# Stick-breaking attention, last head pair: the six copies of the output's inputs go two by two over three tiles instead of three by three over two, and the output units' pieces run a tile later

## The reference, cut to what matters

```python
y_pool = pool_mixer(u, w_pool[i], pool_scale[i])          # 512 channels, done before the attention
o_sb = stick_breaking_attention(q, k, v)                  # 8 heads of 64
y_sb = rms_norm_2(o_sb, ones).reshape(b, s, SB_WIDTH) * g_sb[i]
mix = jnp.concatenate([y_pool, y_sb], axis=-1) @ w_out[i]
h = h + rms_norm_2(mix, g_mix_post[i])
```

## Time and profile before

| | us |
|---|---|
| median of 3 runs | 2429.26 (2428.68 to 2429.6) |
| profiled execution, time | 2429.0 |
| profiled execution, span of the core | 2427.2 |
| PE busy in the span | 2298.8 (95%) |
| DVE, POOL, ACT busy | 1605.5, 1170.5, 1096.1 |
| mean granted TensorE clock | 0.976 |

### The profile page before, as it was taken

One profiled execution on the slowest core, in us unless ns is written; L12 is line 12 of the kernel. 1 busy time (PEld: TensorE's weight loads), 2 busy tenths in 40 slices (PEclk: granted clock), 3 DMA queues, 4 the chain that ended last, 5 costly groups with the idle time before them and its releaser, 6 DMA issues. The chain is left out here.

```text
span 2427.2 us, 28938 instructions
## 1 busy us (share of the span) xinstructions
PE 2298.8 (95%) x10276; PEld 1765.5 (73%) x10276; DVE 1605.5 (66%) x1904; ACT 1096.1 (45%) x1779; POOL 1170.5 (48%) x834
## 2 busy tenths in 40 slices
PE   8988886899999999999999999997999999999999
PEld 6865553777888888788775665583788888888887
DVE  7888884288666666646766666747866665544587
ACT  5145554345545443322326666615666662222342
POOL 1000000257887787878521111232777777777732
PEclk9989997999999999999999999998999999999999
DMA  3211100421443436894310000032466668976412
GB/s 130 69 34 26 29 23 9 148 78 46 180 174 113 182 130 245 318 381 157 126 35 18 27 18 14 27 139 87 173 253 258 253 257 324 360 279 266 149 33 85
DMA packets 89166, 342.90 MB, mean 141 GB/s; under 512 B 22401, under 2 KB 23169, under 8 KB 76097
## 3 DMA queue, kind: packets, MB, share of 16 engines
q1 hardware_dynamic: 88368, 336.65, 36.8%
q10 hardware_dynamic: 656, 4.41, 0.5%
HBM read 224.16 MB, written 116.27 MB: 140 GB/s over the span
## 5 line engine op out<-in xcount | busy, mean ns | idle before, releaser
L1101 PE MATMUL ps<-operand,turn_weights 128*128 128x512 f32 x3192 | 736.3, 392 | 16.3 <-POOL turn_weights L728 5.5
L1101 PEld LDWEIGHTS ps<-operand,turn_weights 128*128 128x128 f32 x3192 | 600.6, 189 | 150.7 <-issue 14.4
L728 POOL TENSOR_TENSOR turn_weights<-turn_raw,turn_weights 128x512 fp32r<-128x512 f32 (+1 forms) x330 | 445.0, 1359 | 225.5 <-ACT turn_weights L1563 224.9
L1101 PE MATMUL ps<-hidden_operand,turn_weights 128*128 128x512 f32 x2268 | 517.5, 390 | 3.3 <-issue 1.4
L1101 PEld LDWEIGHTS ps<-hidden_operand,turn_weights 128*128 128x128 f32 x2268 | 424.8, 188 | 95.8 <-issue 6.0
L2756 DVE TENSOR_TENSOR branch_out<-ps,branch_out 128x1024 f32<-128x1024 f32 x172 | 210.5, 1224 | 201.3 <-PE ps L1101 200.3
L690 POOL TENSOR_TENSOR weight_hi<-weight_raw,zero_col 128x1024 fp32r<-128x1024 f32 (+1 forms) x27 | 54.6, 2023 | 582.1 <-PE ps L1007 409.8
L1563 ACT ACTIVATE turn_weights<-turn_raw 128x512 fp32r<-128x512 f32 (+1 forms) x330 | 204.9, 623 | 267.1 <-PE ps L1101 252.3
L842 PE MATMUL ps<-input_hi,weight_hi 128*128 128x512 f32 x592 | 196.2, 413 | 21.3 <-DVE input_lo L2335 10.4
L842 PE MATMUL ps<-input_lo,weight_hi 128*128 128x512 f32 x656 | 205.9, 395 | 0.0
L842 PE MATMUL ps<-input_hi,weight_lo 128*128 128x512 f32 x592 | 185.3, 395 | 0.0
(11 more groups left out here) (351 smaller groups left out, 3579.9 us busy)
## 6 DMA issues: line engine op xcount, KB each, us to landing
hidden_operand<-hidden_kept SPq DMA_DIRECT2D x91, 1024.0 KB, 7.8
hidden_kept<-hidden_parts SPq DMA_DIRECT2D x54, 1024.0 KB, 8.7
hidden_kept<-hidden_parts SPq DMA_DIRECT2D x27, 1536.0 KB, 6.2
turn_raw<-w_ff SPq DMA_DIRECT2D x40, 512.0 KB, 4.1
turn_raw<-w_mlp SPq DMA_DIRECT2D x32, 512.0 KB, 4.3
turn_raw<-w_mlpd SPq DMA_DIRECT2D x32, 512.0 KB, 4.4
turn_raw<-w_ffd SPq DMA_DIRECT2D x20, 512.0 KB, 4.6
weight_raw<-w_out SPq DMA_DIRECT2D x16, 512.0 KB, 3.6
```

Source lines behind the costliest of these rows:

```text
L728: pool_.tensor_tensor(place(p, 1), place(p, 1, WT) if raw is None else raw, bits(place(p, 0)), ALU.subtract).then_inc(s["st_lo"], 1)
L1101: ins = mm(PS[:, b, :], weights(p, w, k), tokens(p, a, k), start=(FRESH[p] and k == 0 and step == 0), stop=(k == n - 1 and step == 2), ski ...
```

## The change

ACT and DVE copy chunks 0 and 1 in tile 36, 2 and 3 in tile 37, 4 and 5 in tile 38. PE runs piece p in tile 37 + p: tile 37 has none, and piece 11 comes after the block sums of tile 47, directly behind piece 10. DVE's copies of the halves move from odd to even tiles, and the fifth comes after the loop. The high half of the weight split that POOL does in tile 38 waits for the low copy of chunk 5 instead of the low softplus of tile 38.

```diff
@@ POOL, split_beside(m): the high part
                 if p == 10 and c < 3:
                     pool.wait_ge(s["q2_lo"], 4 * c + 6)
+                elif p == 2 and c == 3:
+                    pool.wait_ge(s["mix_lo"], 8 + 6)
                 else:
                     pool.wait_ge(s["sb_sp"], tile + 1)
@@ PE, the loop over the tiles
                 if c < 3:
                     pieces(c, p)
-                elif p:
-                    output_pieces(p)
+                elif p > 1:
+                    output_pieces(p - 1)
+            output_pieces(NP - 1)
             pv_pair(4 * NP - 1)
             output_pieces(NP)
@@ ACT, the loop over the tiles
-                if c == 3 and p in (0, 1, 5):
+                if c == 3 and p in (0, 1, 2, 5):
...
-                    for k in {0: (0, 1, 2), 1: (3, 4, 5), 5: (6,)}[p]:
+                    for k in {0: (0, 1), 1: (2, 3), 2: (4, 5), 5: (6,)}[p]:
                         mix_hi(k, MIX2[k])
@@ DVE, the loop over the tiles
-                elif p % 2 and p > 1 and c == 3:
-                    output_part((p - 3) // 4, c + 1, (p - 3) // 2 % 2)
+                elif p % 2 == 0 and p > 2 and c == 3:
+                    output_part((p - 4) // 4, c + 1, (p - 4) // 2 % 2)
...
-                if c == 3 and p in (0, 1, 5):
-                    for k in {0: (0, 1, 2), 1: (3, 4, 5), 5: (6,)}[p]:
+                if c == 3 and p in (0, 1, 2, 5):
+                    for k in {0: (0, 1), 1: (2, 3), 2: (4, 5), 5: (6,)}[p]:
                         mix_lo(k, MIX2[k], 8)
+            output_part(2, 4, 0)
             decayed(4 * NP - 1)
             summed(4 * NP - 1)
             output_part(2, 4, 1)
```

## The result

| | before | after |
|---|---|---|
| time, median (lowest to highest), us | 2429.43 (2427.04 to 2431.72), 10 runs | 2435.59 (2432.49 to 2438.33), 10 runs |
| ratio, 95% interval | | 1.0027 (1.0018 to 1.0035) |
| profiled execution, time / span, us | 2429.0 / 2427.2 | 2434.8 / 2433.1 |

The change makes the kernel slower by 0.27%; the interval is 4.4 to 8.5 us, the medians stand 6.2 apart. 2435.1 had been forecast, with 2431.0 to 2437.6 as range.

The account below looks back on a forecast made before the run. In the changed stretch DVE, fed by ACT, was taken as the limit, not PE. Terms 2.65 + 2.28 + 0.85 = 5.8 us later gave 2434.8 profiled, with 0.26 for the median 2435.1; range 2431.0 to 2437.6.

Parts of the forecast that it names:

- DVE idle ahead of chunk 4: Tile 38: DVE waits some 2.9 us for ACT's high copy, which stands behind the norm's guess.
- sums of tile 40: PE's sums of tile 40 come 2.65 us late, as `decayed` follows the late subtraction of tile 39.
- piece 3, at the clock it had: Tile 40: piece 3 takes 3.40 us, low clock included, as piece 4 did there before; 2.28 at full clock.
- start of tile 41: Tile 41 begins 2.65 us late; lower bound 1.5, with piece 3 at the full clock.
- tiles 41 to 46: Same order of work, copies moved in step with pieces: 0, up to 2 us more if the clock falls again.
- owed piece and wait for the bank: At the end: one piece owed, 2.28 us, and PE waiting 0.85 for DVE's copy between pieces 10 and 11.
- last product with v: End of the attention: 5.8 us later, a shift that goes through to the kernel's end undiminished.
- The first three tiles: Tiles 36 to 38: fewer low copies ahead bring the CAST of tile 37 1.17 us earlier, tile 38's 2.34.
- The race between POOL and DVE: Tile 39: POOL's split begins before DVE's low subtraction and blocks it; 1.7 us, or 0 if the subtraction wins.
- rival 1: Tile 39: POOL loses to DVE's subtraction, `decayed` 0.95 us late, total 2433.4, or 2432.3 with full clock; chance 0.20.
- Rival 2: Spreading keeps PE fed if the CAST of tile 39 begins by about 1522.3: 7.8 us faster, 2421.4; chance 0.10.
- Rival 3: The clock falls once more in tile 39 or 42: up to 2 us on top, 2437.1; chance 0.14.

Follow-up runs that it names:

- experiment 1: Kernel after with POOL's split in tile 38 released by the low softplus again, as before the change: 2432.34 us, ratio 1.0012.
- experiment 5: Kernel after with pieces 9 and 10 both in tile 46, so pieces 10 and 11 are not neighbours: 2433.66 us, ratio 1.0020.
- experiment 10: Kernel after with POOL's old wait, pieces 9 and 10 both in tile 46, and DVE's copy-out behind `decayed`: 2433.97 us, ratio 1.0023.
- experiment 3: Kernel before with only the pieces, and DVE's copy-out of them, a tile later; copies three by three, POOL's old wait: 2432.38 us, ratio 1.0010.
- experiment 9: Kernel after with DVE's low copies behind the next tile's split and its copy-out behind `decayed`: 2428.97 us, ratio 0.9998.
- experiment 2: Kernel before with only the copies spread two by two over three tiles, pieces and POOL's wait as before: 2434.22 us, ratio 1.0011.
- experiment 4: Kernel before with POOL's new wait alone: 2431.08 us, ratio 1.0005.
- experiment 7: Kernel before with DVE's low copies behind the next tile's split, POOL's old wait: 2426.81 us, ratio 0.9989.

## Why the prediction was right

The time came where it had been put, 0.5 us above the forecast, and by the mechanism of the forecast. Step by step:

| step | predicted | measured |
|---|---|---|
| CAST of tile 37 | 1.17 earlier | 1.14 |
| CAST of tile 38 | 2.34 earlier | 2.28 |
| DVE idle ahead of chunk 4 | about 2.9 | 3.62 |
| POOL behind the last low copy | 0.17 | 0.16 |
| subtraction of tile 39, end | 4.2 late | 4.82 |
| sums of tile 40 | 2.65 late | 3.23 |
| piece 3, at the clock it had | 3.40 | 2.29 |
| start of tile 41 | 2.65 late | 1.80 |
| tiles 41 to 46 | 0 | 0.60 |
| owed piece and wait for the bank | 2.28 + 0.85 | 3.03 |
| last product with v | 5.8 late | 5.43, 5.88 with 0.45 from ahead |

**The first three tiles** went as read from the earlier trace rows, to within 0.06 us. **The idle time of DVE** was 0.7 longer: the clock was low until 1520. PE's low sums of tile 38 began 2.28 earlier than before, as forecast, right behind DVE's subtraction; but from their start to the block sums it took 0.72 us (1517.78 to 1518.50) where it took 0.56 before (1519.61 to 1520.17), and from there to the piece 1.06 instead of 0.58 (1518.50 to 1519.56, before 1520.17 to 1520.75). ACT waits for both, so that its guess ended at 1521.81 rather than 1520.7: 1.64 earlier than before instead of 2.3, the other 0.45 being the later start. That is the one term mis-sized on the way to tile 40, and it explains 3.23 for 2.65.

**The race between POOL and DVE** went as the order in the earlier trace rows said, and rival 1 fell: POOL began 0.16 behind its release, the subtraction 0.23. The Trainium skill, "SBUF — State Buffer", section "Who interferes with whom", holds that an instruction of DVE with two inputs in SBUF contends with one of GpSimd that reads SBUF, and that the order of issue settles who is blocked. The trace agrees: 2.10 here with POOL 0.07 ahead, 0.43 in experiment 1 with POOL out of the way.

**Piece 3** was mis-sized the other way. I had taken the low clock of the earlier trace rows; in this execution the level fell earlier, in tile 39 (0.57 from 1528 to 1532), and piece 3 ran at the full one: 1.11 less, and 0.32 less in the low sums ahead of it. The start of tile 41 lay at 1.80, between the bound of 1.5 and the 2.65 taken. In experiment 5, the same program up to tile 46, the piece took 3.51, and in experiment 10 it ran at the low level too, so either is to be had: that it went this way in the profiled execution is luck, and made up for the terms that were too small.

**"Tiles 41 to 46. Same order of work ... 0"** is the step that was wrong, by 0.60. The order of DVE's work had changed: its copy of a half unit now falls in the even tiles, and in tile 42 it stands ahead of `decayed`, on which PE's block sums wait (0.56). The prediction had moved the copies "in step with pieces" and put nothing on what stands behind them. Experiment 3 has the same gap without the copies, and experiment 10 hasn't with the copy-out behind `decayed`.

**The end** cost what had been forecast, and experiments 3 and 5 show the wait for the bank (0.79) to belong to the shifted pieces and to fall to 0.16 when pieces 10 and 11 are not neighbours. The owed piece counts in full here because in front, where DVE sets the pace, leaving a piece out won nothing; in experiment 3 tile 41 began 2.86 earlier instead. **Nothing was caught up** behind the attention.

**Rival 2, faster by PE fed,** failed at the point that had been named: the CAST of tile 39 would have had to begin by 1522.3 and began at 1525.07, or 1524.62 without the 0.45 from ahead. Experiment 9 goes further than the prediction: with the CAST no longer behind the copies, spreading with the shift of pieces still gives no gain, while the old three and three in that order give 0.23%. **Rival 3, the clock falling once more,** came true in one of its two places: it fell in tile 39, where piece 2 took 3.78 us (1528.37 to 1532.15), and not in tile 42. It added nothing to the time, as PE then still waited 0.94 for DVE's CAST of tile 40, and the fall in tile 40 that the forecast held didn't come. The rival that the clock alone makes the time was not tested by holding the clock; against it stand the gaps with DVE as releaser, and that of the 3.23 at the sums of tile 40 about 0.6 came through the clock, by ACT's guess.

That the errors compensated has to be said: 0.6 too little up to tile 40, 1.4 too much in piece 3 and the sums ahead of it, 0.6 too little behind it, and 0.45 from ahead of the stretch, which no reading of this change could give. **Open** remains how the total splits among the parts in the timing: the single parts measured 1.0011, 1.0010 and 1.0005, which together make 1.0026 beside the 1.0027 of the whole, but each with an interval of some ±0.0009. That they add up is no evidence for the parts: in experiment 2 it is piece 2 that waits, in experiment 4 another tile's subtraction, and neither happens in the kernel after. Experiments 1, 5 and 10 do not come down by the amounts seen in their profiles.

## What to carry to other kernels

Before work is spread over more slots, look at what it stands ahead of in its engine's queue: here three copies behind the CAST (0.9989 by the order alone, 0.9977 with POOL's wait moved to suit) beat both three and two copies ahead of it, since PE's gap there was a wait for the CAST and not for the copies. A filler that is shifted by one slot is owed at the end; it costs its whole length where leaving it out in front won nothing, as here, and less where it did, and its neighbours at the end can meet over one bank: price the first and the last slot by themselves. When a wait is moved to another releaser, ask which instruction comes directly behind that releaser on an engine that shares something with the waiting one.

## What was not expected of the hardware

POOL's weight split, released by a DVE instruction, stopped the next subtraction with both inputs in SBUF every time that it began first: 2.10 us for 0.43 in the kernel after, 2.26 for 0.69 in experiment 4, 2.36 for 0.67 in experiment 9, and 4.05 for 2.35 in experiment 7. The stopped instruction ended 0.28 us after POOL's in the kernel after and 0.55 after it in experiment 9. The other order shows once in the rows above: in experiment 7 POOL began 0.25 behind a low copy and took 2.72 instead of 1.89. A CAST, which has one input, is stretched too: the one of tile 39 took 0.65 beside POOL before and 0.29 in the kernel after.

Runs of one kernel lie up to 9 us apart (2429.07 to 2437.87 in experiment 1), where the three runs shown ahead of the prediction lay within 0.9. In the profiled executions the granted clock falls in other tiles from one kernel to the next, and even the CAST of tile 36, ahead of which all kernels are the same, begins anywhere from 1496.78 to 1503.01 us. The Trainium skill, "TensorE: Matmul & The Clock Gate", section "What's actually happening", says that the number of slow matmuls differs from run to run of one kernel. The traces agree in kind: over the code that all kernels have in common, up to 1490 us, the time lost to the low level (one minus the granted clock, added up) differs from 37.5 to 41.0 us between the twelve profiled executions. But it doesn't order the starts of that CAST: the earliest (1496.78) has 37.5, and so has the kernel after (1499.92), the latest (1503.01) 39.3. What moves the starts stays open.

A consequence for reading: times of single executions can't be compared here to better than about 6 us. What could be compared was a stretch counted from a common instruction, and the gaps in it with their releasers.
